# Three projection units side by side through four input tiles, then one by one through the other four

## What the kernel computes

```
x = x + gate * nsa_mixer(norm(x))        # q, k, v, z projections; compressed, selected, windowed attention; output projection
x = rms_norm(x + gate * dilated_mixer(norm(x)), final_g)   # 4 x 1024 projections, dilated attention, output projection
x = x + gate1 * (merged(window attention, short conv) @ w_out)
x = x + gate2 * peer(norm(x))            # 2048 query columns, product keys, top 16 experts of 16384 for each of 8 heads
```

## Time and profile before

| | us |
|---|---|
| median of 3 runs | 2418.85 (2411.94 to 2422.42) |
| the profiled execution, its own time | 2416.59 |
| its span | 2414.7 |
| PE busy in the span | 2269.5 (94%) |
| DVE / POOL / ACT busy | 1545.9 / 1310.6 / 916.4 |

### The profile page before, as it was taken

The page is one execution under the profiler, slowest core; times in us unless marked ns, Lnnn a source line. Parts: engine busy times, 40 slices in busy tenths (PEclk is TensorE's granted clock), DMA queues, the critical chain, the costliest instruction groups (busy, mean ns, idle before and its releaser), DMA issues. The chain is left out here.

```text
span 2414.7 us, 32126 instructions
## 1 busy us (share of the span) xinstructions
PE 2269.5 (94%) x11911; PEld 1978.8 (82%) x11911; DVE 1545.9 (64%) x2911; ACT 916.4 (38%) x1517; POOL 1310.6 (54%) x691
## 2 busy tenths in 40 slices
PE   4999999889999878998999999999998999999998
PEld 4798787767778766776899999999997888878787
DVE  6416878544315565543089999999993676766665
ACT  2223655332237332442233333455553333333332
POOL 0522110136431224233358878766665899999996
PEclk9999999899999889998999999999999999999999
DMA  7233556322220211122248888899997899999996
GB/s 260 87 123 114 176 166 212 102 73 96 88 70 1 70 53 64 42 70 66 83 132 265 290 260 290 266 381 333 338 348 288 304 347 341 339 351 341 345 343 239
DMA packets 164474, 492.40 MB, mean 204 GB/s; under 512 B 15072, under 2 KB 64608, under 8 KB 162912
## 3 DMA queue, kind: packets, MB, share of 16 engines
q1 hardware_dynamic: 107872, 305.79, 37.4%
q0 software_dynamic: 36864, 134.23, 15.3%
q10 hardware_dynamic: 19584, 50.34, 5.4%
HBM read 437.87 MB, written 52.43 MB: 203 GB/s over the span
## 5 line engine op out<-in xcount | busy, mean ns | idle before, releaser
L2190 POOL TENSOR_TENSOR t_split<-t_raw,t_split 128x1024 fp32r<-128x1024 f32 x256 | 628.9, 2458 | 151.1 <-ACT t_split L2117 147.5
L240 POOL TENSOR_TENSOR w_split<-ring,w_split 128x1024 fp32r<-128x1024 f32 x113 | 273.9, 2431 | 554.4 <-ACT w_split L232 543.2
L2083 PE MATMUL ps<-t_split,w_split 128*128 128x512 f32 x2304 | 531.5, 392 | 16.0 <-DVE w_split L2358 12.0
L2049 PE MATMUL ps<-h_hi,t_split 128*128 128x384 f32 x2048 | 537.5, 339 | 6.5 <-POOL t_split L2190 3.6
L2083 PEld LDWEIGHTS ps<-t_split,w_split 128*128 128x128 f32 x2304 | 431.8, 188 | 115.6 <-POOL t_split L2190 12.4
L264 PE MATMUL ps<-h_hi,w_split 128*128 128x512 f32 x1440 | 471.4, 403 | 10.2 <-POOL w_split L240 10.2
L2117 ACT ACTIVATE t_split<-t_raw 128x1024 fp32r<-128x1024 f32 x256 | 270.3, 1057 | 367.8 <-DMA t_raw<-v_table 219.0
L2049 PEld LDWEIGHTS ps<-h_hi,t_split 128*128 128x128 f32 x2048 | 373.9, 189 | 8.6 <-POOL t_split L2190 5.4
L2049 PE MATMUL ps<-h_lo,t_split 128*128 128x384 f32 x1024 | 344.2, 336 | 0.0
L264 PEld LDWEIGHTS ps<-h_hi,w_split 128*128 128x128 f32 x1440 | 273.2, 190 | 76.4 <-issue 15.3
L264 PE MATMUL ps<-h_lo,w_split 128*128 128x512 f32 x720 | 282.7, 393 | 0.0
(11 more groups left out here) (315 smaller groups left out, 3289.1 us busy)
## 6 DMA issues: line engine op xcount, KB each, us to landing
ring<-w_stream SPq DMA_DIRECT2D x219, 512.0 KB, 3.4
t_raw<-u_table SPq DMA_DIRECT2D x128, 512.0 KB, 4.6
t_raw<-v_table SPq DMA_DIRECT2D x128, 512.0 KB, 5.0
gelu_scratch<-e_gel ACTq DMA_DIRECT2D x128, 192.0 KB, 5.1
gates_scratch<-arena ACTq DMA_DIRECT2D x8, 3072.0 KB, 13.0
arena<-gelu_scratch SPq DMA_DIRECT2D x32, 768.0 KB, 5.7
arena<-gates_scratch SPq DMA_DIRECT2D x32, 768.0 KB, 8.8
xT<-x_in SPq DMA_DIRECT2D x2, 1024.0 KB, 11.1
```

Source lines behind the costliest of these rows:

```text
L240: pool.tensor_tensor(w_split[:, i % RS, 1, :], ring[:, n % R, :], w_split[:, i % RS, 0, :].bitcast(F32), ALU.subtract).then_inc(lo_done, 1)
L2049: mm = pe.matmul(ps[:, 6 + n % 2, 0:NT], t_split[:, n % RAWS, u, k * P:(k + 1) * P], h_parts[h][:, k, P:T], start=(k + u + h == 0), stop=( ...
L2083: mm = pe.matmul(ps[:, 2 * i + half, :], w_split[:, b % 2, w, at:at + P], t_split[:, m % RAWS, v, half * 512:(half + 1) * 512], start=(n + ...
L2190: pool.tensor_tensor(t_split[:, m % RAWS, 1, :], t_raw[:, m % RAWS, :], t_split[:, m % RAWS, 0, :].bitcast(F32), ALU.subtract).then_inc(t_ ...
```

## The change

Only the body of `feature_group` changes. Through the first four input tiles (`half`) the units still go side by side. Then comes `between`, where there is one. Through the other four tiles unit 0 goes alone and waits for each tile, then unit 1 and then unit 2, which wait for nothing more. Each unit counts `piece_used` up at its own last matmul, as before. Matmuls, waits and semaphore updates are the same in number, and each bank adds up in the same order.

```diff
             w = {}
-            for at, k in enumerate(order):
-                if between and at == KD // 2:
-                    between(pe)
+            half = KD // 2
+
+            def product(at, j):
+                for a, b in HI_LO:
+                    k = order[at]
+                    mm = pe.matmul(ps[:, banks[j], :], w[j][:, a, k * P:(k + 1) * P], src[b][:, k, :],
+                                   start=(at + a + b == 0), stop=(at == KD - 1 and a == 1))
+                return mm
+
+            for at in range(half):
                 src_ready.wait(pe, at + 1)
-                for j, bank in enumerate(banks):
+                for j in range(len(banks)):
                     if at == 0:
                         w[j] = piece_ready(pe, pieces[j])
-                    for a, b in HI_LO:
-                        mm = pe.matmul(ps[:, bank, :], w[j][:, a, k * P:(k + 1) * P], src[b][:, k, :],
-                                       start=(at + a + b == 0), stop=(at == KD - 1 and a == 1))
-                    if at == KD - 1:
-                        mm.then_inc(piece_used, 1)
+                    product(at, j)
+            if between:
+                between(pe)
+            for j in range(len(banks)):
+                for at in range(half, KD):
+                    if j == 0:
+                        src_ready.wait(pe, at + 1)
+                    mm = product(at, j)
+                mm.then_inc(piece_used, 1)
```

## The result

| | before | after |
|---|---|---|
| median us | 2414.74 (13 runs, 2408.74 to 2423.72) | 2400.54 (13 runs, 2391.11 to 2410.46) |
| ratio | 1 | 0.9938, 95% interval 0.9924 to 0.9951 |
| span of the profiled execution | 2414.7 | 2392.6 |

The changed kernel is 0.62% faster, by the ratio 15.0 us of 2414.7 (11.8 to 18.4 by the interval), by the medians 14.2. The forecast was a gain of 16.4 us and a time of 2402.5. From line 290 on, source lines move by 11: L587 is the L576 of before, L710 the L699, L1635 the L1624; the matmul of a group is L276.

A forecast was written before the change was run, and what follows sets the result against it. PE decides in the projections, idling 10.2 us for POOL's low part. Six gains from 1.15 to 4.22 us sum to 16.4, giving 2400.2 on the profiled execution and 2402.5 as median, range 2394 to 2414.

The forecast's parts named there:

- The six stalls: PE's waits behind the groups of e, f, g, wq, dq and q2 go; 16.4 us, low clock included.
- 1.15 forecast: At q2, PE's wait for ACT's square of unit 0 goes and the whole chain moves by 1.15 us.
- rival 4: Before unit 3, POOL's wait isn't for unit 0, or unit 0 waits for tiles; time stays 2418; chance 0.06.
- The low clock behind f and wq: Half clock in the units behind f and wq goes with the stalls; bounds 0 and about 3.1 us, 3.1 taken.
- rival 2: At f and wq stalls go, but low clock stays or falls elsewhere; gain 13.3 us, time 2405.6; chance 0.22.
- 4.09: Projection f: stall of 2.53 us plus 1.56 us of low clock in unit 3 go, together 4.09 us.
- rival 3: Something behind piece 3's low part is late; e, f, g, wq give back up to 2.5 us each, 2412.5; chance 0.11.
- Late inputs: In four groups (L772, dq, q2, wq), unit 0 alone waiting for tiles costs 0, at worst 1.92 us each, 7.7.

The follow-up runs named there:

- run 1: The changed kernel's matmul order, but all units of a group count piece_used up together at the group's last matmul; 2435.64 us, ratio 1.0072.
- run 4: The changed kernel with six input tiles side by side instead of four, then one by one through two; 2409.62 us, ratio 0.9970.
- run 2: The changed kernel with the new order only in output projections e, f and g, the other groups as before; 2407.18 us, ratio 0.9952.
- run 5: The changed kernel with one input tile side by side instead of four, except projection g, which keeps four; 2405.88 us, ratio 0.9950.

## Why the prediction was right

**The six stalls.** Right in place and size. Behind e, f, g and wq the distance from the group's end to unit 3 went from 2.53, 2.53, 2.54 and 2.44 to 0; dq's first round from 8.02 to 6.35; the first sum of q2 follows its group at once, where it stood 1.16 behind it, and the stage is 1.22 shorter (1.15 forecast). Runs 1 and 4 show that it is the release of unit 0's place against 3.9 us of splitting: rival 4 falls with run 4, where the stall is as long as that difference says.

**The low clock behind f and wq.** I counted its 3.1 us as gone, with rival 2, that it stays or falls elsewhere, at 0.22. Right behind the groups it is gone, and the table over all traces shows the link. But the profiled pair gives half of it back. Behind the column sums of f the kernel before has a low stretch of 6.83 us, the changed one of 17.06 us (13.9 of it before the stage ends). That part of the stage, with the norm in it, takes 16.11 us instead of 14.68, 1.43 more, which is why f gave 2.63 instead of 4.09. In runs 2 and 5, where the low stretch is 6.8 us, stage f takes 58.25 and 58.30 us, the 4.1 less that were forecast. The windows, before and then after:

```profile
854.38:869.06 14.68, 7.11 (x50) 6.83 (x48) 6.34 (x22) 5.87 (x9) 7.10 (x4) 0.77 0.24 78
859.40:866.23 6.83, 3.03 (x14) 3.03 (x15) 2.82 (x13) 2.21 (x5) 5.45 (x3) 0.50 0.23 80
```

```profile
839.45:855.56 16.11, 8.54 (x49) 8.15 (x48) 6.33 (x22) 5.87 (x9) 7.09 (x4) 0.57 0.24 75
841.69:858.75 17.06, 9.49 (x37) 8.43 (x37) 8.77 (x26) 6.08 (x9) 7.09 (x4) 0.50 0.28 94
```

From the group of e to the peer stage the mean clock is 0.95 in both traces:

```profile
466.39:1221.34 754.95, 684.25 (x3237) 563.14 (x3235) 319.82 (x602) 264.13 (x543) 252.86 (x122) 0.95 0.19 63
```

```profile
459.12:1199.68 740.56, 679.37 (x3238) 562.07 (x3236) 323.10 (x602) 265.27 (x543) 250.85 (x122) 0.95 0.19 64
```

So how much of the 3.1 us is saved on average is not settled: the measured gain, 11.8 to 18.4 us, holds both the 16.4 of the forecast and the 13.3 of rival 2.

I had taken the Trainium skill's rule ("TensorE: Matmul & The Clock Gate", section "Why this matters for your kernels") as the ground of rival 2: it warns of longer gaps only, so gaps as short as those of 2.4 to 2.5 us should leave the clock alone. The traces here disagree: 6 of 8 such stalls were followed by a unit at a low clock. The four of run 1, 3.8 to 3.9 us, were too, but they are of the length that the rule warns of.

**The time itself** came out nearer than the sum behind it. The forecast of 2402.5 starts from a median of three runs, 2418.85, and the median of 13 is 2414.74, 4.1 less. The gain by the medians was 14.2 instead of 16.4, 2.2 less. The two errors partly cancel, and that is luck.

**The wait moves on (rival 3).** It did not. DVE's addition and the split of piece 4 were in time everywhere. DVE's running total was stretched to 2.5 us in e beside a split of POOL, as it was to 2.4 before the change, without anyone waiting for it.

**Late inputs.** Cost 0, as said. With one tile side by side they cost 0.8 to 1.9 us in each of five groups. So four tiles lies between 1 (inputs late) and 6 (release late); 2, 3 and 5 were not run.

**What the prediction did not see** is the collision of DVE and POOL ahead of dq and wq. It did not enter the sum, since it is there with either kernel, but in the profiled pair it took 2.3 us from stage e, of which 1.5 came back in dq, whose group took 17.79 us instead of 19.33 because fewer of its first matmuls ran at half pace (5 steps of 0.43 us against 13); a reader of these two traces alone would have found e "not improved". It was in the trace of before: the rows of L576 go up to 2.93 us where 0.75 is normal, and I used only the landing times of the last tiles.

## What to carry to other kernels

Units that share a resource and run side by side all give it back at their end. Going side by side is worth it only for as long as the inputs arrive more slowly than one unit uses them; after that, finish one unit first, and leave at least as much work behind it as the refill takes (here 3.9 us of splitting against 5.44 us of matmuls). A stall in front of dense matmuls costs more than its length, since the clock may drop behind it. And a gain of half a per cent is read from the stages of the trace, not from the span.

## What the runs showed of the hardware

- A stall of PE of 2.4 to 2.5 us was followed by a stretch at half clock (1.2 of 2.4 GHz) in the unit behind in 6 of 8 cases, one of 3.8 to 3.9 us in 4 of 4, one of 1.1 to 1.2 us in none of 4. The half clock costs 1.5 to 3 us in the unit behind.
- A DVE instruction with two SBUF inputs (L587, 0.75 us) took 2.93 us when the next of POOL's subtractions of two SBUF inputs began some 0.05 us after it (13 cases in the ten traces). It took 2.20 us when it began in the middle of one (3 cases). In all 16 it ended 0.54 to 0.55 us after the split. The split kept its 2.3 us in the first kind; in the second it took 2.8, having begun beside DVE's subtraction before. DVE's L582, with one input in PSUM, kept its 0.7 us beside the same split. The Trainium skill, "SBUF — State Buffer", section "SBUF: two separate sides", says that such a DVE instruction and one of GpSimd use one shared pair of ports, and that whichever starts second is blocked until the other has ended. The ends agree with a blocked DVE. The order does not show, since in the 13 cases DVE's row starts some 0.05 us before the split that it waits out, while the split before still has 0.08 us to go.
- PE's pace does not depend on whether neighbouring matmuls go to one PSUM bank or change it after every three: 0.227 us in both orders at the full clock.
